# Weights split in place: the low part of a unit written over its raw slot, and the slot refilled once TensorE has used it

## The reference

```
h = rms_norm(x, g_mix);  q, k, v = split(h @ w_in)      # 2048 x 6144
x = x + mixed @ w_out                                    # 2048 x 2048
x = x + (silu(conv(g) + b) * u) @ w_down                 # g, u = h @ w_up, 2048 x 11264; 5632 x 2048
h = h + 0.5 * rmsnorm((silu(u @ w_gate) * (u @ w_up)) @ w_down, g_post)    # twice, 2048 x 5632 and back
```

## Time and profile before

| What | Value |
|---|---|
| Median of three runs | 3703.81 us |
| The runs | 3722.18, 3690.02, 3703.81 us |
| Profiled execution, its span | 3721.3 us, nearest to the run of 3722.18 |
| TensorE busy (matmuls / weight loads) | 3336.9 / 2861.2 us |
| VectorE busy | 2198.9 us |
| ScalarE busy | 1572.3 us |
| Read from HBM | 591.70 MB, 160 GB/s over the span |
| DMA busy, share of 16 engines | 50.8% (the queue of the unit loads) |
| Granted TensorE clock, mean | 0.938 of full |

### The profile page before, as it was taken

The page is one execution under the profiler, slowest core; times in us unless marked ns, Lnnn a source line. Parts: engine busy times, 40 slices in busy tenths (PEclk is TensorE's granted clock), DMA queues, the critical chain, the costliest instruction groups (busy, mean ns, idle before and its releaser), DMA issues.

```text
span 3721.3 us, 49866 instructions
## 1 busy us (share of the span) xinstructions
PE 3336.9 (90%) x18334; PEld 2861.2 (77%) x18334; DVE 2198.9 (59%) x2263; ACT 1572.3 (42%) x1863; POOL 211.8 (6%) x89
## 2 busy tenths in 40 slices
PE   6996598799999997999999988985688999999966
PEld 5885486688888886788888876864467888888855
DVE  5555575666666456556555456575666555555466
ACT  3443353444544433444444333445334444443333
POOL 1000120200000001000000001000110000000011
PEclk9997798899999999999999998987799999999978
DMA  5662154366666554555665654642145666655533
GB/s 170 211 187 82 45 159 136 110 188 185 185 185 185 187 186 138 163 185 185 196 190 188 193 178 122 186 136 81 46 147 153 185 185 185 184 188 186 186 104 108
DMA packets 321784, 595.23 MB, mean 160 GB/s; under 512 B 18228, under 2 KB 41940, under 8 KB 321684
## 3 DMA queue, kind: packets, MB, share of 16 engines
q1 hardware_dynamic: 313808, 587.27, 50.8%
q10 hardware_dynamic: 7876, 6.63, 0.6%
HBM read 591.70 MB, written 2.13 MB: 160 GB/s over the span
## 4 chain that ended last, share of the span: by engine, by line
PE 85%; DVE 10%; issue 2%; ACT 1%; DMA 1%; POOL 0%; POOLq 0%; DVEq 0%; ACTq 0%; SPq 0%
PE acc L421 54%; PE acc L423 27%; DVE OPR L1202 2%; DVE wl L1111 1%; DVE T L1217 1%; DVE X L1222 1%; ACT wh L745 0%; PE acc L393 0%; PE acc L460 0%; DVE S L1190 0%; DMA raw<-in_w_in 0%; DVE T L1125 0%; PE acc L584 0%; DVE S L1261 0%; PE acc L482 0%
## 5 line engine op out<-in xcount | busy, mean ns | idle before, releaser
L421 PE MATMUL acc<-OPR,wh 128*128 128x512 f32 x6480 | 2324.6, 403 | 129.6 <-DVE OPR L1202 84.2
L1111 DVE TENSOR_TENSOR wl<-raw,wh 128x1024 fp32r<-128x1024 f32 x1112 | 1403.6, 1270 | 1266.8 <-ACT wh L745 1266.0
L423 PE MATMUL acc<-OPR,wl 128*128 128x256 f32 x6480 | 1832.4, 283 | 0.0
L745 ACT ACTIVATE wh<-raw 128x1024 fp32r<-128x1024 f32 x1112 | 1167.7, 1058 | 1511.4 <-PE acc L423 1487.1
L421 PEld LDWEIGHTS acc<-OPR,wh 128*128 128x128 f32 x6480 | 1239.9, 191 | 448.6 <-issue 102.5
L423 PEld LDWEIGHTS acc<-OPR,wl 128*128 128x128 f32 x6480 | 1244.8, 192 | 0.0
L421 PE MATMUL acc<-HR,wh 128*128 128x512 f32 x2272 | 798.6, 397 | 3.3 <-DVE T L1125 2.3
L423 PE MATMUL acc<-HR,wl 128*128 128x256 f32 x2272 | 635.3, 280 | 0.0
L421 PEld LDWEIGHTS acc<-HR,wh 128*128 128x128 f32 x2272 | 426.6, 188 | 108.2 <-DVE T L1125 2.9
L423 PEld LDWEIGHTS acc<-HR,wl 128*128 128x128 f32 x2272 | 428.3, 189 | 0.0
L1125 DVE TENSOR_TENSOR T<-acc,T 128x1024 f32<-128x1024 f32 (+1 forms) x111 | 134.4, 1211 | 14.1 <-ACT T L763 14.0
(11 more groups left out here) (257 smaller groups left out, 1274.5 us busy)
## 6 DMA issues: line engine op xcount, KB each, us to landing
raw<-in_w_up SPq DMA_DIRECT2D x176, 512.0 KB, 3.9
raw<-in_ff_w_gate SPq DMA_DIRECT2D x176, 512.0 KB, 3.7
raw<-in_ff_w_up SPq DMA_DIRECT2D x176, 512.0 KB, 4.5
raw<-in_ff_w_down SPq DMA_DIRECT2D x176, 512.0 KB, 4.4
raw<-in_w_in SPq DMA_DIRECT2D x170, 512.0 KB, 3.7
raw<-in_w_down SPq DMA_DIRECT2D x88, 512.0 KB, 4.7
raw<-in_w_out SPq DMA_DIRECT2D x64, 512.0 KB, 4.5
raw<-in_w_ple_gate SPq DMA_DIRECT2D x32, 512.0 KB, 3.8
```

The source lines that it names most:

```text
L421: pe.matmul(acc[:, b + t, :], wh[:, s, col:col + P], x, start=(u == 0 and k == 0), stop=False)
L423: mm = pe.matmul(acc[:, b + t, 0:T], wl[:, s, col:col + P], x[:, 0, :], start=False, stop=last)
L745: act.activation(wh[:, s, :], raw[:, s, :], ACT.Copy).then_inc(hi_done, 1)
L1111: dve.tensor_tensor(wl[:, s, :], raw[:, s, :], wh[:, s, :].bitcast(F32), ALU.subtract)\
```

## The change

The tile `wl` loses its own memory and is laid over `raw`: the low part of a unit is written where its raw weights were. So a slot of `raw` is in use until TensorE is done with the unit, and the load into it waits for `units_used` instead of `lo_done`. The waits of ScalarE, VectorE and TensorE are as they were. All tiles placed behind `wl` lie 16 KB per partition lower.

```diff
-        for name, floats in (("raw", 4096), ("wh", 4096), ("wl", 4096), ("x", 4096), ("op", 8192),
+        for name, floats in (("raw", 4096), ("wh", 4096), ("x", 4096), ("op", 8192),
                              ("h", FC * 512), ("vec", NVEC), ("t1", 1024), ("t2", 1024),
...
         raw = sb("raw", "raw", [P, SLOTS, 1024])
         wh = sb("wh", "wh", [P, SLOTS, 1024], F32R)
-        wl = sb("wl", "wl", [P, SLOTS, 1024], F32R)
+        wl = sb("wl", "raw", [P, SLOTS, 1024], F32R)
...
                 if u >= SLOTS:
-                    sp.wait_ge(lo_done, more + (u - SLOTS + 1))
+                    sp.wait_ge(units_used, more + (u - SLOTS + 1))
```

## The result

The changed kernel takes 3948.86 us (median of 4 runs, 3940.50 to 3950.40) against 3701.35 us for the kernel before in the same comparison (3690.02 to 3722.18): a ratio of 1.0649 [1.0613, 1.0685], 247 us more. 3910 was forecast, with a range of 3845 to 4010. The profiled execution has a span of 3947.1 us, 225.8 above that of before.

The account below looks back on a forecast made before the run. TensorE, busy 90% of the span, was taken to bound the kernel, with losses at the joints. Terms of 80 + 30 + 67 + 16 + 13 = 206 us over the 3703.8 us median gave 3910 us, range 3845 to 4010.

Parts of the forecast that it names:

- What the load waits for: DMA queue: its wait turns from VectorE's low split to TensorE's use of unit u-4, again 1108 times.
- D: Delay from the use that starts a load to the split: landing plus about 0.1 us for signals, 3.8 to 4.6 us.
- quicker landings: Rival: loads no longer issued in bursts land half a microsecond sooner at 69 places, 35 us less, 3875 us; chance 0.09.
- page estimate: Landing of 512 KB from a fixed 2 us plus bytes over 436 GB/s: 3.2 us, giving a sum of about 150 us.
- Odd ends: 33 odd block ends of feed-forward pairs: stalls of 2.35 us (22) and 2.55 us (11), 80 us in all.
- the slack of 1.45: Odd block ends: the first split behind the hidden values ends 9.6 us after the block; TensorE wants it after 11.1 us.
- Even ends: 20 even block ends in the two layers without a convolution: stall of 1.5 us each, 30 us in all.
- the slack of 3.1: Even block ends: the second unit's low split ends 8.0 us after TensorE finishes the block, leaving 3.1 us.
- Folds and projection ends: 8 folds behind splits and 8 projection ends: each wait grows by all of D, 16 x 4.2 = 67 us.
- Preparations and odd places: Six operand preparations at 2.7 us, 16 us; six odd places with cover not worked out, half of 0 to D, 13 us.
- Mid-block and the write in place: Three units, 8.3 us, cover a 6.1 to 6.9 us chain inside blocks; the in-place subtraction changes nothing: no cost.
- The clock: Rival: the clock falls in new stalls, about 2 us each; odd ends add 66 us (3976), with even ends 106 (4016); chance 0.12.

Follow-up runs that it names:

- e1: The kernel before with only the load's wait changed, to the use of unit u-4, low part keeping its own tile: 3947.21 us, ratio 1.0654.
- e2: The changed kernel with eight raw slots, low parts still in place, a load waiting for the use of unit u-8: 3697.85 us, ratio 0.9978 to before.
- e8: The kernel before, early loads kept, with the last split of every block moved behind the end-of-block work: 3677.74 us, ratio 0.9926.
- e4: The changed kernel with the last unit's splits at odd block ends of feed-forward pairs moved later on ScalarE and VectorE: 3843.05 us, ratio 1.0361 to before.
- e5: The eight-slot ring of e2, but a load waits for the use of unit u-4, as in the changed kernel: 3953.23 us, ratio 1.066 to before.
- e6: The eight-slot ring of e2, but a load waits for the use of unit u-6: 3710.73 us, ratio 1.003 to before.
- e12: e8 with the last low split of down, ff1_down, w_out2 and ff2_down moved behind the next norm's fold on VectorE: 3679.96 us, ratio 0.9944 to before.

## Why the prediction was right, point by point

**What the load waits for.** Right: all 1108 waits turned, and e1 gives the whole loss with that line alone.

**D.** 3.7 us at the folds, just under the predicted 3.8 to 4.6. Counted over all block ends it is a little more: at the 33 odd ends the last split starts 4.11 us after TensorE's next unit, against 0.21 in the kernel before, so 3.9; at the 20 even ends 3.8. The load is issued some 0.2 to 0.35 us after that unit's start, where I had allowed 0.1 in all for the signals. I had listed quicker landings as a rival, with 9%, since the bursts would be gone. That rival's mechanism came true: 3.6 us for every matrix, 3.6 or 3.7 in e2, and 3.7 to 4.5 again in e8, where loads once more follow VectorE's low splits. Its price was small (24 us of the sum of gaps) and other costs outweighed it. The page estimate from "The DMA setup-cost knee" of the Trainium skill's "SBUF — State Buffer", 3.2 us, is still under the measured 3.6; its sum of 150 us is under the 182 of the gaps.

**Odd ends.** Right in size to a microsecond, 80.3 us. With 3.9 us and the slack of 1.45 the stall is 2.4 to 2.5, as in the terms. The longest one, 3.15 us at the last odd end of the second layer, had a load that landed late, 4.3 us from issue to split. Here are that load and its split, and those of the end shown above (whose split starts at 1812.64, 3.7 us behind its load):

```profile
1808.96 3.26 SPq L335 DMA_DIRECT2D raw<-in_ff_w_gate  x2
...
2102.26 3.15 SPq L335 DMA_DIRECT2D raw<-in_ff_w_down  x2
...
2106.60 1.06 ACT L745 ACTIVATE wh<-raw 128x1024 fp32r<-128x1024 f32 x1 [2.28 <-DMA raw<-in_ff_w_down]
```

e4 shows the chain.

**Even ends.** Mis-sized: 0.36 to 1.0 us each in place of 1.5, but for one of 2.0 us, 13.5 in place of 30. With D at 3.7 to 3.8 the slack of 3.1 leaves 0.6 or 0.7. The one of 2.0 us had a load that was issued at 1636.20 and took 5.2 us:

```profile
1641.46 1.06 ACT L745 ACTIVATE wh<-raw 128x1024 fp32r<-128x1024 f32 x1 [3.27 <-DMA raw<-in_ff_w_up]
```

The slack was right; the term took the up matrix's 4.5 us over into a schedule that no longer had the bursts behind it.

**Folds and projection ends.** Right in mechanism: + 3.7 and + 3.8 us. Two places didn't pay in full: the fold of ple_gate grew by 2.1, and the last projection's end shrank by 0.6.

**Preparations and odd places.** Taken as one sum with the four other projection ends, right (45.4 against 46), but the odd places rest on a half taken, and no run takes them apart. Within the trace, the gaps of the six preparations grew by 15.2 us, against 16 forecast.

**Mid-block and the write in place: nothing.** Right, by e1, e2 and e5.

**The clock.** The forecast gave nothing in the sum and 12% to a fall behind each odd end, 66 us. The truth lies between: 12 of the 33 odd ends and one even end are followed by a stretch at 0.50, at 1.5 to 2.7 us each, 22 us (the 2 us a fall that the rival gave was a fair price); 33 over the whole kernel, with the first pairs behind the stalls. In the middle of the second layer they are the ends at 1772, 1919 and 2066 us, every third. The Trainium skill, "TensorE: Matmul & The Clock Gate", section "HAM oscillation", tells of a kernel in which every wait for a DMA brought the lower clock. Here it came behind about one in three of the odd ends' stalls, and that one in three is the term that the sum lacked. With it the sum is 182.4 + 32.8 = 215 of 226 us; the last pair ahead of each stall makes up the other 11.

**The median.** The forecast was 206 us over the median, and 247 came: 226 by the profiles, and 21 because the profile of before was a slow-paced run. I noted those 18 us in the prediction and took them for spread. The changed kernel's profile is as slow-paced (34% quick pairs against 32%), while the median run of before would need about two thirds, an estimate from the 56 us. So the 21 us are a difference of pace between the two medians, and whether the change has a part in it isn't shown. That the total came so near has some luck in it: the gaps were put 24 us too high, and 33 + 11 us at the stalls and 21 of pace were not in the sum.

## What to carry to other kernels

Letting a tile's last reader free it costs the landing time only where the distance to the next need is shorter: work out the slack at each joint (block end, fold, projection end), since in mid-block the other slots hide it. One unit of lead more, from 4 slots to the use of u-5, took the loss from 6.6% to 0.9%, and two left no gap of the change and a time that a measurement can't tell from before. At a joint, look for work that doesn't belong to the chain but stands in it in an engine's order; moving the last split of each block behind the block's own work made the kernel before 0.7% faster, and where the split was moved past the first step only, it stood in the way of the second.

## What the runs showed that I had not expected

**Two paces at one clock.** At a granted clock of 1.00 the pairs of matmuls in a projection start every 0.3466 or every 0.3533 us. The pace nearly always holds until TensorE waits, if only for some hundredths of a microsecond, and is then one or the other: the traces of before and e6 switch 13 and 20 times, that of after, with its 167 gaps, 60 times. Over the kernel it is worth 56 us, and that is as wide as the spread of the kernel before, 3680.77 to 3735.11 us over all comparisons: its profiles give 3683 us for all pairs quick and 3739 for none. The changed kernel, with many short stretches, spreads over 10 us only, in four runs. What chooses the pace is open.

**Landings in company.** 512 KB took 3.6 us when each load was let go by a use, one unit apart, and up to 4.8, by matrix (median, `w_down` in e12), when loads were let go by VectorE's low splits, two or three of which follow each other at once behind a block's end. No run changes the spacing alone, so the cause is argued; and single loads one unit apart took 4.2 and 5.2 us in the changed kernel.
